# Down biases folded into the gate-weighted sums, and these sums issued one chunk later

## The reference

```
logits = x @ w_router + b_router              # 320 x 32
top_val, top_idx = top_k(logits, 4)
gates = softmax(top_val)                      # 4 gates for a token
for each token t and each chosen expert e:
    gu  = x[t] @ w_gate_up[e] + b_gate_up[e]  # 1024 -> 2048
    g   = min(gu[:1024], 7); up = clip(gu[1024:], -7, 7)
    hdn = (up + 1) * (g * sigmoid(1.702 * g))
    out = hdn @ w_down[e] + b_down[e]         # 1024 -> 1024
y[t] = sum over the chosen e of gates[t, e] * out[t, e]
```

## Time and profile before

| | |
|---|---|
| median of 3 runs | 1234.11 us |
| the profiled execution, its own time | 1232.76 us |
| its span, first to last instruction | 1231.1 us |
| granted clock of TensorE, mean | 0.999 |
| PE busy | 1217.2 us, 99% of the span, 7773 instructions |
| DVE, ACT, POOL busy | 475.5, 188.8, 246.8 us |
| DMA moved | 440.51 MB, 358 GB/s over the span |
| chain that ended last | PE 74%, DMA 7%, DVE 1% |
| L1061, gate and up products | 471.7 us busy in 2048 instructions |
| L1106, down products | 226.8 us busy in 1024 instructions |
| L1025, the combines | 106.7 us busy in 384 instructions |
| L1092, the down bias products | 64 instructions of 403 ns, pairs side by side |

### The profile page before, as it was taken

How to read it: one execution, slowest core, us unless ns; L and a number is a source line. 1 busy time by engine, 2 the same in 40 slices (tenths; PEclk the granted TensorE clock), 3 DMA queues, 4 the chain that set the end, 5 groups by cost and what they waited for, 6 DMA issues and landing times.

```text
span 1231.1 us, 21141 instructions
## 1 busy us (share of the span) xinstructions
PE 1217.2 (99%) x7773; PEld 557.3 (45%) x7774; DVE 475.5 (39%) x918; ACT 188.8 (15%) x321; POOL 246.8 (20%) x438
## 2 busy tenths in 40 slices
PE   9999999999999999999999999999999999999997
PEld 7666666778433333333433333333334333333332
DVE  6878967435522222222322222222233222222224
ACT  4741024334300000100000000000000000000002
POOL 2077860000211111111111111111111211111100
PEclk9999999999999999999999999999999999999999
DMA  8324232895999999999999999999999999999995
GB/s 234 103 69 130 85 122 75 261 397 209 378 416 425 428 428 428 408 435 429 434 432 428 434 433 427 437 431 429 434 431 429 437 429 430 435 425 427 427 427 230
DMA packets 61189, 440.51 MB, mean 358 GB/s; under 512 B 11838, under 2 KB 40290, under 8 KB 42884
## 3 DMA queue, kind: packets, MB, share of 16 engines
q1 hardware_dynamic: 59940, 439.50, 86.6%
q10 hardware_dynamic: 1216, 0.56, 0.2%
HBM read 438.18 MB, written 1.87 MB: 357 GB/s over the span
## 4 chain that ended last, share of the span: by engine, by line
PE 74%; DMA 7%; DVE 1%; ACT 0%; issue 0%; SPq 0%; DVEq 0%; ACTq 0%
PE psum L1061 33%; PE psum L1106 16%; DMA big<-in_w_gate_up_dram 7%; PE psum L1025 7%; PE psum L1011 5%; PE psum L616 4%; PE psum L594 3%; PE psum L907 2%; PE psum L1071 1%; PE psum L1092 1%; DVE acc L2063 0%; PE psum L923 0%; ACT big L1353 0%; PE psum L936 0%; PE psum L978 0%
## 5 line engine op out<-in xcount | busy, mean ns | idle before, releaser
L1061 PE MATMUL psum<-big 128*64 128x512 f32 x2048 | 471.7, 597 | 2.5 <-DMA big<-in_w_gate_up_dram 2.4
L2013 DVE TENSOR_TENSOR acc<-acc,psum 128x512 f32<-128x512 f32 (+1 forms) x192 | 123.1, 682 | 569.3 <-PE psum L1025 567.1
L1061 PEld LDWEIGHTS psum<-big 128*64 128x64 f32 x2048 | 138.0, 136 | 303.6 <-issue 287.1
L1106 PE MATMUL psum<-big 128*64 128x512 f32 x1024 | 226.8, 595 | 0.0
L616 PE MATMUL psum<-big 128*128 128x320 f32 x576 | 161.1, 436 | 0.0
L1535 POOL COPY big<-uT 96x64 bf16 x32 | 7.5, 234 | 647.8 <-PE psum L1092 647.1
L1106 PEld LDWEIGHTS psum<-big 128*64 128x64 f32 x1024 | 70.7, 137 | 134.1 <-issue 127.9
L616 PEld LDWEIGHTS psum<-big 128*128 128x128 f32 x576 | 107.5, 190 | 47.9 <-issue 5.5
L1025 PE MATMUL psum<-big 64*128 64x512 f32 (+1 forms) x384 | 106.7, 632 | 0.0
L1402 ACT ACTIVATE big<-big 128x512 f32<-128x512 f32 x32 | 20.2, 632 | 538.2 <-DVE big L2036 538.2
L1544 POOL TENSOR_SCALAR big<-cst,big 128x128 f32<-128x128 f32 x96 | 75.1, 793 | 7.7 <-POOL big L1539 7.7
(11 more groups left out here) (296 smaller groups left out, 843.9 us busy)
## 6 DMA issues: line engine op xcount, KB each, us to landing
big<-in_w_gate_up_dram SPq DMA_DIRECT2D x40, 4096.0 KB, 22.5
big<-in_w_gate_up_dram SPq DMA_DIRECT2D x42, 2048.0 KB, 15.5
big<-in_w_down_dram SPq DMA_DIRECT2D x20, 4096.0 KB, 23.3
big<-in_w_down_dram SPq DMA_DIRECT2D x19, 2048.0 KB, 16.6
big<-in_w_in_dram SPq DMA_DIRECT2D x18, 1024.0 KB, 5.4
big<-in_w_gate_up_dram SPq DMA_DIRECT2D x12, 1024.0 KB, 8.6
big<-in_w_down_dram SPq DMA_DIRECT2D x8, 1024.0 KB, 9.3
big<-in_w_s_glu_dram SPq DMA_DIRECT2D x8, 512.0 KB, 4.0
```

What stands on the lines that cost most here:

```text
L1061: mm = pe.matmul(psum[SLOT * hf:SLOT * hf + SLOT, GB + gu, :], xeT[:, 4 * (c % 2) + 2 * k + c // 2, :], hidden(big[:, base:base + FF], hf) ...
L1106: mm = pe.matmul(psum[SLOT * hf:SLOT * hf + SLOT, DB, :], hT[:, m, c, :], big[:, base:base + 512], start=False, stop=(c == DN_CHUNKS - 1 a ...
L2013: v.tensor_tensor(x, x, psum[0:n, CB + hf, :], ALU.add).then_inc(S("added"), 1)
```

## The change

`b_down` is no longer split and no longer multiplied in the blocks. It is loaded once, in f32, into `osb` (32 rows for each half of its columns), and `pt` gets the whole gate table of the tokens, turned by twenty 32x32 transposes on DVE. So the three sums of block 0, which added zeros, now add gates times bias rows. `xh`, which lay in `osb`, moves to where `bd3` lay. The three combines of every block come one chunk later, after c1, c2 and c3, and DVE's third `add` goes to the end of its loop. The transposes stand between the gate table and `last_rest(2)`, which was ahead of both.

```
-        bd3 = cut(w.take(D // 2).bitcast(BF16), 1, D)[0:3 * NE, 0]
+        xh = w.take(D // 2)
...
-                        sp.dma_start(bias_d[r32], a["b_down"][0]).then_inc(S("bias_landed"), 16)
...
             sp.wait_ge(S("ss"), 5)
+            for hf in range(2):
+                sp.dma_start(osb[SLOT * hf:SLOT * hf + NE, :], a["b_down"][0][:, hf * 512:(hf + 1) * 512]).then_inc(S("bias_landed"), 16)
             expert_half(sp, 0, 1, 0)
...
-            pe.wait_ge(S("bias_cast"), 6)
+            pe.wait_ge(S("bias_cast"), 3)
+            pe.wait_ge(S("bias_landed"), 5 * 16)
...
-                        if c < 3:
-                            combine(g, c)
+                        if c > 0:
+                            combine(g, c - 1)
...
-                    for hf in range(2):
-                        mm = pe.matmul(psum[SLOT * hf:SLOT * hf + SLOT, DB, :], csel, bd3[:, hf * 512:(hf + 1) * 512],
-                                       start=True, stop=False, skip_group_check=True)
-                    mm.then_inc(S("csel_used"), 1)
...
-                                               start=False, stop=(c == DN_CHUNKS - 1 and m == 3), skip_group_check=True)
+                                               start=(c + m == 0), stop=(c == DN_CHUNKS - 1 and m == 3), skip_group_check=True)
...
-                nc.scalar.copy(bd3[0:n], bias_d[0:n]).then_inc(S("bias_cast"), 1)
...
-            pool.sem_inc(S("pt_ready"), 1)
+            pool.sem_inc(S("zeros_set"), 1)
...
-                v.tensor_tensor(bias_d[0:n], bias_d[0:n], bd3[0:n], ALU.subtract).then_inc(S("bias_rest"), 1)
...
             first_rest(2)
-            last_rest(2)
             for i in range(3):
                 gate_table(i)
             dve.sem_inc(S("gates_tab"), 1)
+            dve.wait_ge(S("zeros_set"), 2)
+            for i, (t0, n) in enumerate(TILES):
+                for at in range(0, n, NE):
+                    for hf in range(2):
+                        do.start(v.transpose(pt[SLOT * hf:SLOT * hf + NE, t0 + at:t0 + at + NE], tab[at:at + NE, :, 3 + i]))
+            do.wait()
+            dve.sem_inc(S("pt_ready"), 1)
+            last_rest(2)
...
-                    for i in range(3):
-                        add(g, i)
+                    add(g, 0)
+                    add(g, 1)
...
                     v.tensor_copy(flat(hT[:, 2:4]), psum[:, UB, 0:2 * P]).then_inc(S("hi_copied"), 1)
+                    add(g, 2)
```

More of the change, by code:

```diff
@@ L251, in hybrid_stream_step @@
         square2 = cut(m2[:, 0:3 * D], 3, D)
-        bd3 = cut(w.take(D // 2).bitcast(BF16), 1, D)[0:3 * NE, 0]
+        xh = w.take(D // 2)
         nfb = nmb
         SCRB = 5
-        bias_gu, bias_d = m2[0:3 * NE, 3 * CHUNK:3 * CHUNK + 2 * FF], nmb[0:3 * NE, :]
+        bias_gu = m2[0:3 * NE, 3 * CHUNK:3 * CHUNK + 2 * FF]
         BIAS_ROWS = (3 * NE, 2 * NE, NE)
@@ L270, in hybrid_stream_step @@
         one2 = pw[:, 0, 0:SLOT]
-        xh = osb
         same = cut(sm[:, 0:NE * TOPK], NE, TOPK)
@@ L1070, in expert @@
                                     for hf in range(2):
-                                        pe.matmul(psum[SLOT * hf:SLOT * hf + SLOT, GB + gu, :], csel, hidden(bgu3[0:3 * NE, gu * FF:(gu + 1) * FF], hf),
-                                                  start=False, stop=False, skip_group_check=True)
+                                        mm = pe.matmul(psum[SLOT * hf:SLOT * hf + SLOT, GB + gu, :], csel, hidden(bgu3[0:3 * NE, gu * FF:(gu + 1) * FF], hf),
+                                                       start=False, stop=False, skip_group_check=True)
+                                mm.then_inc(S("csel_used"), 1)
                         mm.then_inc(S("chunks_used"), 1)
@@ L1309, in bias_part @@
                 if k == 0:
-                    act.wait_ge(S("bias_landed"), 6 * 16)
+                    act.wait_ge(S("bias_landed"), 3 * 16)
                 else:
-                    act.wait_ge(S("bias_rest"), 2 * k)
+                    act.wait_ge(S("bias_rest"), k)
                 n = BIAS_ROWS[k]
                 nc.scalar.copy(bgu3[0:n], bias_gu[0:n]).then_inc(S("bias_cast"), 1)
-                nc.scalar.copy(bd3[0:n], bias_d[0:n]).then_inc(S("bias_cast"), 1)
             for i in range(16):
@@ L1834, in bias_left @@
                 n = BIAS_ROWS[k]
-                dve.wait_ge(S("bias_cast"), 2 * k)
+                dve.wait_ge(S("bias_cast"), k)
                 v.tensor_tensor(bias_gu[0:n], bias_gu[0:n], bgu3[0:n], ALU.subtract).then_inc(S("bias_rest"), 1)
-                v.tensor_tensor(bias_d[0:n], bias_d[0:n], bd3[0:n], ALU.subtract).then_inc(S("bias_rest"), 1)
             for j in range(T_ML):
@@ L1890, in first_rest @@
                 if i == 0:
-                    dve.wait_ge(S("bias_cast"), 6)
+                    dve.wait_ge(S("bias_cast"), 3)
                 if i == 1:
```

## The result

| | median us | lowest to highest | runs |
|---|---|---|---|
| before, on the same chip | 1233.53 | 1232.62 to 1234.25 | 6 |
| changed | 1238.63 | 1236.92 to 1239.20 | 6 |

The ratio is 1.004, with a 95% interval of 1.003 to 1.005: the change makes the kernel 5.1 us slower. I had forecast 1235.0 us (1231.6 to 1237.6). The profiled execution took 1238.44 us, 5.7 us more than that of before, and its span is 1236.5 us against 1231.1. The profiled execution of before was 0.8 us faster than its median, that of the changed kernel 0.2.

The account below looks back on a forecast made before the run. The prediction took PE and the weight stream as nearly equal limits, the stream setting the pace. +0.45 us from the late restart and +0.46 at the end made +0.9 on 1234.11: 1235.0 us, range 1231.6 to 1237.6.

Parts of the forecast that it names:

- Two limits on each other: Middle of the loop: PE and weight stream nearly equal, 28.19 against 29.2 us a block; saved PE time returns as waits.
- Bias product worth 0: Every block: dropping the 0.30 us product gains 0, since it covered the next weight load's wait for ACT.
- Order worth 0.15 a block: Every block: c1 directly behind c0 saves one change of tile shape, -0.15 us, bounded at 0 to -0.30.
- Twenty transposes at 0.18: Start, on DVE: 0.18 us each, the middle of 0.11 and 0.23, so 3.6 us (2.2 to 4.6).
- rival C: Start: transposes at 0.27 us stall it three times, down products 3.0 us late, 1236.7 us in all; chance 0.16.
- The estimate of 190 ns: Start: price of one transpose from the skill's fixed latency of about 150 cycles; 3.8 us for twenty.
- Block 0 late by 1.35 us: Block 0: gather waits 1.5 us for POOL's one-hot matrices, so down products start at 335.4, 1.35 us late.
- What the stream makes of it: Weight stream: restarts 1.35 us late; at its pause at 510 PE is 0.45 late, so +0.45 us.
- The end, +1.06: Behind the last chunk PE waits for: two combines instead of one, +1.06 us, net +0.46 after the blocks' savings.
- The slack of 1.2 us: Block 31: c2 landed at 1198.1, PE took it at 1199.27; coming 0.6 us earlier, PE would not wait.
- Four more blocks give back 4 x 0.15: Last four blocks, behind block 27's c2: each saves 0.15 us, bringing the end's +1.06 to +0.46.

Follow-up runs that it names:

- e2: Kernel before with only the combines one chunk later and DVE's third add at the end of its loop; bias products kept: 1234.07 us, ratio 1.0005.
- e3: Kernel before without the two bias products of each block, down biases left out: 1233.23 us, ratio 0.9998.
- g2: Kernel before with the three turns of the gate rows made thirteen times in block 0, 6.85 us more PE work: 1240.5 us, ratio 1.0057.
- h2: Kernel before with SyncE's first rows of expert 2 held until block 0's down products are done, no added compute: 1235.76 us, ratio 1.0019.
- f2: Changed kernel with last_rest(2) ahead of the gate table again, and ten transposes plus one copy for twenty transposes: 1233.99 us, ratio 1.0005.
- e1: Changed kernel without the twenty transposes, down biases left out: 1233.7 us, ratio 1.0002.
- e4: Kernel before with only the gate table and twenty transposes ahead of last_rest(2), into a buffer nobody reads: 1238.87 us, ratio 1.0045.
- f6: Kernel before without block 0's three empty combines, block 0 ahead of PE's loop and experts 29 to 31 behind it, old combine order: 1231.15 us.
- f1: Changed kernel with last_rest(2) ahead of the gate table and transposes again, all twenty transposes kept: 1237.32 us, ratio 1.0032.
- f3: Kernel before without block 0's three empty combines, PE's first turn of four experts written out ahead of its loop: 1290.01 us, ratio 1.0458.
- f5: Kernel before without block 0's empty combines, combines later except in each turn's last expert, block 0 ahead of PE's loop, experts 29 to 31 behind: 1230.71 us.

## Why the prediction was wrong, point by point

- **Two limits on each other; PE time in the loop is worth nothing.** Right. e2 shows 28.04 us a block and no gain.
- **Bias product worth 0.** Right, by e3, and the wait for ACT stands in its place (13.5 us in 32 for 6.2).
- **Order worth 0.15 a block.** Right to 0.01, by e2. The Trainium skill, TensorEngine Tiling (Array Packing), section "Key Properties", says that a change of tiling mode drains TensorE; the trace agrees in kind, and gives it the size of 0.15 us (c0 and c1 together 6.87 instead of 7.01); that the 0.15 is a drain isn't shown.
- **Twenty transposes at 0.18.** Here the prediction failed first. They take 0.225 each, 0.255 apart: 5.10 us for 3.6. I had weighed the two nearest operations by their elements down to 0.11 and 0.23, and so put the measured distance outside my own bounds; L1909's 0.27, taken whole, was the better neighbour, and I had it only in rival C. The estimate of 190 ns, from the Trainium skill, VectorE: DVE Perf Modes, section "The TRN2 errata", was too low as well; the measurement decides.
- **Block 0 late by 1.35 us.** It was 5.15, 3.8 more. Of that 1.5 are the transposes (5.10 for 3.6), which alone gives 2.9, near rival C's 3.0. Another 1.4 come from the fall of the clock, which stood nowhere in the prediction: from the gather's start to the down products 4.25 us passed, forecast were 2.87 (the fall cost 1.5, and 0.1 came back with the bias products). About 0.5 more since the whole start lay that much later (c0 at 313.11 for 312.63; over the experiments c0 starts at 312.6 to 313.3, so it needn't be the change's). The last 0.4 are GpSimd's: from its loop's entry to the end of its second matrices it took 10.10 us for 9.49, and its entry followed VectorE 0.26 sooner.
- **What the stream makes of it.** I had put +0.45. The mechanism was right and its size followed from the start. By the prediction's own steps 5.15 - 6 x 0.15 = 4.25 us, and 4.3 came out at the landing of block 31's c2: the issue at 335.93 came 5.25 late, the DMA engines stood for nearly 4 us, and at 515 PE and stream were 4.35 late. g2 and h2 show it without the change's parts.
- **The end, +1.06.** The combine behind the last landing was there (1212.30), and 1.06 us is in the trace. What it cost in time isn't shown: f2 and e2 are 0.8 and 0.6 us over B, e1 0.2, none clear of zero. The slack of 1.2 us that I read for c2 of block 31 wasn't there: e2 takes it at 1199.33 behind a wait. "Four more blocks give back 4 x 0.15" failed with it: blocks 28 to 30 took 28.04 us each and gave 0.45 back, and block 31 lost it again to its wait (28.47 us).
- **The rivals.** C was the right one, with its place, a price of 1236.7 and two of its three stalls: the first combine waited 1.53 us and the gather 1.83, but the second combine didn't wait, as VectorE's first `add` began at 323.61, 0.93 us after its last operation where 2.25 was assumed. With the clock's 1.5 us C would have been 1238.2. I gave it 0.16 on the strength of the interpolation above.

Sum as measured: 4.3 at the landing + 1.06 = 5.3 us in the span of the two profiles. By the medians, 5.1 us, of which the start's edits in f2 take away 4.3 and leave 0.8, not told from zero. That the parts of the 4.3 divide just so isn't shown: of the clock's share there is no kernel with the waits and without the fall.

## What to carry to other kernels

Where two chains end within a few us of each other, an operation's price isn't its duration but whose start it holds: 5.1 us of transposes on an engine that is busy 39% of the span cost 5.4 us (e4), and 0.30 us in each of 32 blocks on the busiest engine cost nothing. Look at what the first block does that it needn't: three empty combines were worth 2.4 us (f6), more than everything the change tried. For an operation the trace doesn't have, take the nearest small one whole and don't scale it down by elements: here VectorE operations of 32 to 128 elements a partition all cost 0.22 to 0.27 us.

## What the runs showed of the hardware

- Small DVE operations: a 32 x 32 transpose of f32 takes 0.225 us and follows its neighbour at 0.255. A copy of 320 elements a partition takes 0.32 (f2).
- PE's clock fell to the lower level after a wait of 3.56 us (e4), and after 1.53 and 1.83 us with work between (changed kernel); in f1, after 2.8 us in one, the profiled execution shows no fall, though its mean clock is 0.998 and four of the six runs have 0.997. It cost 1.5 us in the changed kernel and 1.7 in e4.
- A copy of four experts ahead of PE's loop in f3 went with instructions fetched anew at every return (81 packets for 21, 43.2 us of PE standing). g2, with four experts ahead of the loop too, and f5 and f6, with one ahead and three behind, moved 27 packets and had no such pauses. What decides between them wasn't found.
